# A convolution/attention trunk on one core: shorter bias rows, and LayerNorm's channel sums by pairwise additions

## What is computed

```python
# layer 0: conformer convolution module
a, b, z = split(rmsnorm(x) @ w_in)                 # 2048 channels each
u = a * sigmoid(b)
c = causal_depthwise_conv(u, conv_w, width 31) + conv_b
mu  = mean(c, over channels)
var = mean((c - mu)**2, over channels)
cn  = (c - mu) * rsqrt(var + eps) * ln_g + ln_b
x   = x + (silu(cn) * silu(z)) @ w_out
# layer 1: three attention groups (window, dilation) = (128,1), (512,4), (2048,16)
bias = rel_bias[t5_bucket(distance * dilation)]    # one value per head and distance
score = q.k * scale + bias, masked where distance < 0 or outside the window
```

## Time and profile before

| | |
|---|---|
| median of 3 runs | 1447.31 us (1447.19 to 1447.31) |
| profiled execution, own time | 1447.93 us |
| its span, first to last instruction | 1446.0 us |
| PE busy | 1427.4 us (99%) |
| DVE / ACT / POOL busy | 895.6 (62%) / 720.3 (50%) / 384.9 us (27%) |
| mean granted TensorE clock | 0.998 |
| layer 0 with its projection | about 0 to 390 us |

### The profile page before, as it was taken

The page is one execution under the profiler, slowest core; times in us unless marked ns, Lnnn a source line. Parts: engine busy times, 40 slices in busy tenths (PEclk is TensorE's granted clock), DMA queues, the critical chain, the costliest instruction groups (busy, mean ns, idle before and its releaser), DMA issues.

```text
span 1446.0 us, 23852 instructions
## 1 busy us (share of the span) xinstructions
PE 1427.4 (99%) x8915; PEld 1312.8 (91%) x8915; DVE 895.6 (62%) x1503; ACT 720.3 (50%) x1167; POOL 384.9 (27%) x169
## 2 busy tenths in 40 slices
PE   7999999999999999999999999999999999999997
PEld 6999999988889989999899998999989999899886
DVE  3899999622556566565665656656566565665633
ACT  6344444675644455444554445544455444554643
POOL 5888888798300000000000000000000000000785
PEclk9999999999999999999999999999999999999999
DMA  9676766556697666676666766667666676664652
GB/s 276 179 196 179 196 184 192 166 196 199 181 267 191 174 185 174 179 191 174 185 174 178 192 174 185 174 177 193 174 185 174 178 192 174 185 174 164 235 194 87
DMA packets 455088, 268.49 MB, mean 186 GB/s; under 512 B 4491, under 2 KB 437211, under 8 KB 454668
## 3 DMA queue, kind: packets, MB, share of 16 engines
q1 hardware_dynamic: 454572, 267.11, 65.2%
q10 hardware_dynamic: 480, 0.90, 0.2%
HBM read 263.70 MB, written 4.29 MB: 185 GB/s over the span
## 4 chain that ended last, share of the span: by engine, by line
PE 97%; ACT 1%; DVE 1%; issue 0%; ACTq 0%; DVEq 0%
PE bank L429 29%; PE bank L431 14%; PE bank L436 6%; PE bank L407 6%; PE bank L406 6%; PE bank L405 6%; PE bank L437 6%; PE bank L438 6%; PE bank L458 4%; PE bank L456 4%; PE bank L457 4%; PE bank L1463 1%; PE bank L1478 1%; PE bank L1447 1%; ACT mem_a L661 0%; PE bank L1476 0%
## 5 line engine op out<-in xcount | busy, mean ns | idle before, releaser
L370 POOL TENSOR_TENSOR w_lo<-raw,w_hi 128x1024 fp32r<-128x1024 f32 x159 | 381.5, 2409 | 1033.7 <-ACT w_hi L361 1033.3
L361 ACT ACTIVATE w_hi<-raw 128x1024 fp32r<-128x1024 f32 x382 | 399.5, 1061 | 419.7 <-PE bank L438 131.1
L370 DVE TENSOR_TENSOR w_lo<-raw,w_hi 128x1024 fp32r<-128x1024 f32 x224 | 268.4, 1222 | 187.7 <-ACT w_hi L361 185.5
L429 PE MATMUL bank<-mem_b,w_hi 128*128 128x512 f32 x1024 | 360.8, 398 | 0.0
L431 PE MATMUL bank<-mem_b,w_lo 128*128 128x256 f32 x1024 | 286.4, 280 | 0.0
L429 PE MATMUL bank<-mem_a,w_hi 128*128 128x512 f32 x768 | 270.9, 397 | 0.1
L429 PEld LDWEIGHTS bank<-mem_b,w_hi 128*128 128x128 f32 x1024 | 192.7, 188 | 45.7
L436 PE MATMUL bank<-mem_a,w_hi 128*128 128x256 f32 x768 | 216.4, 282 | 1.6 <-DVE mem_a L962 1.6
L431 PE MATMUL bank<-mem_a,w_lo 128*128 128x256 f32 x768 | 214.9, 280 | 0.0
L437 PE MATMUL bank<-mem_a,w_hi 128*128 128x256 f32 x768 | 214.8, 280 | 0.0
L438 PE MATMUL bank<-mem_a,w_lo 128*128 128x256 f32 x768 | 213.7, 278 | 0.0
(11 more groups left out here) (186 smaller groups left out, 1741.3 us busy)
## 6 DMA issues: line engine op xcount, KB each, us to landing
raw<-w_kv_dram SPq DMA_DIRECT2D x96, 1024.0 KB, 6.0
raw<-b_w_in_dram SPq DMA_DIRECT2D x64, 1024.0 KB, 7.0
raw<-a_w_in_dram SPq DMA_DIRECT2D x47, 1024.0 KB, 5.8
raw<-a_w_out_dram SPq DMA_DIRECT2D x16, 1024.0 KB, 5.0
raw<-b_w_out_dram SPq DMA_DIRECT2D x16, 1024.0 KB, 5.1
bias<-bias_dram SPq DMA_DIRECT2D x16, 384.0 KB, 6.5
x_sb<-x_dram SPq DMA_DIRECT2D x4, 512.0 KB, 5.8
resid_dram<-x_sb SPq DMA_DIRECT2D x1, 2048.0 KB, 10.0
```

Source lines behind the costliest of these rows:

```text
L361: nc.scalar.activation(w_hi[:, stream.half_slot(half), :], raw[:, slot, part:part + HALF], ACT.Copy).then_inc(hi_done, 1)
L370: eng.tensor_tensor(w_lo[:, stream.half_slot(half), :], raw[:, slot, part:part + HALF], w_hi[:, stream.half_slot(half), :].bitcast(F32), A ...
L429: nc.tensor.matmul(dst[:, :], w_hi[:, slot, k * P:(k + 1) * P], both_parts(source, kt), start=(kt == 0), stop=False)
```

## The change

The bias table has 256 columns per group, for distances 0 to 255 alone. POOL fills the whole of `bias_vec` with the mask value at its start, PE makes the rows of groups 0 and 1 in one product of 512 columns and those of group 2 in one of 256, both after slab 1, and DVE copies them between the constants in two operations, both ahead of the convolution.

The two times four reductions are replaced by eight additions of SBUF tensors each: 128x512 for the two halves of four tiles, 128x512 into the running pair of sums, and at the end 128x256. One product each remains for the mean and the variance. Each addition that needs the one before it waits for `pair_done`.

```diff
-            sp.wait_ge(vec_copied, NG)
+            sp.wait_ge(vec_copied, 2)
             sp.dma_start(bias_dram.ap(), bias_vec).then_inc(vec_stored, 16)
...
+            nc.gpsimd.memset(bias_vec, MASKED).then_inc(vec_masked, 1)
...
+            def add_channels(stat, q, tiles, done):
+                before = 7 * stat + max(0, 2 * q - 1)
+                halves = ch_sum[:, 2:4, :] if q == 0 else ch_sum[:, 0:2, :]
+                if q > 0:
+                    dve.wait_ge(pair_done, before)
+                nc.vector.tensor_tensor(halves, tiles[:, 0:2, :], tiles[:, 2:4, :], ALU.add).then_inc(pair_done, 1)
+                if q > 0:
+                    dve.wait_ge(pair_done, before + 1)
+                    nc.vector.tensor_tensor(ch_sum[:, 2:4, :], ch_sum[:, 2:4, :], ch_sum[:, 0:2, :],
+                                            ALU.add).then_inc(pair_done, 1)
+                if q == 3:
+                    dve.wait_ge(pair_done, before + 2)
+                    nc.vector.tensor_tensor(ch_sum[:, 0, :], ch_sum[:, 2, :], ch_sum[:, 3, :],
+                                            ALU.add).then_inc(done, 1)
...
-                        nc.vector.tensor_reduce(ch_sum[:, q, :], conv[:, 4 * q:4 * q + 4, :].rearrange("p k s -> p s k"),
-                                                AX.X, ALU.add).then_inc(ch_summed, 1)
+                        add_channels(0, q, conv[:, 4 * q:4 * q + 4, :], ch_summed)
...
-            def copy_vec(g):
-                dve.wait_ge(vec_made, g + 1)
-                nc.vector.tensor_copy(bias_vec[:, g * BIAS_W:(g + 1) * BIAS_W], bank[6 + g % 2][0:HEADS, :]
-                                      ).then_inc(vec_copied, 1)
+            def copy_vec(groups):
+                n = len(groups)
+                dve.wait_ge(vec_masked, 1)
+                dve.wait_ge(vec_made, groups[0] // 2 + 1)
+                by_group = bias_vec.rearrange("h (g e) -> h g e", g=NG)
+                made = bank[6 + groups[0] // 2][0:HEADS, 0:n * S].rearrange("h (g e) -> h g e", g=n)
+                nc.vector.tensor_copy(by_group[:, groups[0]:groups[0] + n, S - 1:2 * S - 1], made).then_inc(vec_copied, 1)
...
-            copy_vec(0)
-            copy_vec(1)
+            copy_vec((0, 1))
+            copy_vec((2,))
...
-                if c == 1:
-                    copy_vec(2)
...
-                nc.vector.tensor_reduce(ch_sum[:, q, :], squares[:, q, :, :].rearrange("p k s -> p s k"),
-                                        AX.X, ALU.add).then_inc(sq_summed, 1)
+                add_channels(1, q, squares[:, q, :, :], sq_summed)
...
-                for g in {1: (0, 1), 3: (2,)}.get(j, ()):
-                    if g == 2:
-                        pe.wait_ge(vec_copied, 1)
-                    nc.tensor.matmul(bank[6 + g % 2][0:HEADS, :], rel, buckets[:, g * BIAS_W:(g + 1) * BIAS_W],
-                                     start=True, stop=True).then_inc(vec_made, 1)
+                    for n, cols in enumerate((2 * S, S)):
+                        nc.tensor.matmul(bank[6 + n][0:HEADS, 0:cols], rel, buckets[:, 2 * n * S:2 * n * S + cols],
+                                         start=True, stop=True).then_inc(vec_made, 1)
...
-                    pe.wait_ge(vec_copied, NG)
-                    for q in range(4):
-                        pe.wait_ge(ch_summed, q + 1)
-                        mm = nc.tensor.matmul(bank[6][:, 0:S], mean_w[:, :], ch_sum[:, q, :], start=(q == 0), stop=(q == 3))
-                    mm.then_inc(mean_ready, 1)
+                    pe.wait_ge(vec_copied, 2)
+                    pe.wait_ge(ch_summed, 1)
+                    nc.tensor.matmul(bank[6][:, 0:S], mean_w[:, :], ch_sum[:, 0, :], start=True,
+                                     stop=True).then_inc(mean_ready, 1)
...
-                    for q in range(4):
-                        pe.wait_ge(sq_summed, q + 1)
-                        mm = nc.tensor.matmul(bank[7][:, 0:S], mean_w[:, :], ch_sum[:, q, :], start=(q == 0), stop=(q == 3))
-                    mm.then_inc(var_ready, 1)
+                    pe.wait_ge(sq_summed, 1)
+                    nc.tensor.matmul(bank[7][:, 0:S], mean_w[:, :], ch_sum[:, 0, :], start=True,
+                                     stop=True).then_inc(var_ready, 1)
```

More of the change, by code:

```diff
@@ L259, in build @@
         rel = raw[0:BUCKETS + 1, 0, NG * BIAS_W:NG * BIAS_W + HEADS]
-        buckets = raw[0:BUCKETS + 1, 0, 0:NG * BIAS_W]
+        buckets = raw[0:BUCKETS + 1, 0, 0:NG * S]
         bias_vec = gate[0:HEADS, 0:NG * BIAS_W // S, :].rearrange("p k s -> p (k s)")
@@ L281, in build @@
         rows_turned, param_ready = sem("rows_turned"), sem("param_ready")
+        vec_masked, pair_done = sem("vec_masked"), sem("pair_done")
         vec_made, vec_copied, vec_stored = sem("vec_made"), sem("vec_copied"), sem("vec_stored")
@@ L1536, in bucket_table @@
 def bucket_table():
-    table = np.zeros((BUCKETS + 1, NG, BIAS_W), np.float32)
+    table = np.zeros((BUCKETS + 1, NG, S), np.float32)
     exact = BUCKETS // 2
     for g, (window, dil) in enumerate(GROUPS):
[L1542 to L1545, removed]
+        for dist in range(S):
+            if dist % dil or dist > window:
+                table[BUCKETS, g, dist] = 1.0
                 continue
@@ L1549, in bucket_table @@
                 bucket = exact + int(math.log(dist / exact) / math.log(MAX_DISTANCE / exact) * (BUCKETS - exact))
-            table[min(bucket, BUCKETS - 1), g, e] = 1.0
-    return table.reshape(BUCKETS + 1, NG * BIAS_W)
+            table[min(bucket, BUCKETS - 1), g, dist] = 1.0
+    return table.reshape(BUCKETS + 1, NG * S)
 def kernel(**inputs):
```

## The result

| | before | after |
|---|---|---|
| median, 6 runs each on one chip | 1447.31 us (1447.07 to 1447.71) | 1453.71 us (1453.44 to 1454.01) |
| profiled execution / its span | 1447.93 / 1446.0 us | 1453.44 / 1451.6 us |
| mean granted TensorE clock | 0.998 | 0.996 |

The ratio is 1.0043, with a 95% interval of 1.0033 to 1.0053: slower by 6.4 us. The forecast was +3.8 (1451.1), its range went up to 1453.9, and the rival "POOL comes first" stood at 1453.1.

The account below looks back on a forecast made before the run. PE, busy 99% of the span, was taken as the bound. Mean +2.9 (bias advance included), clock +2.2 and variance -1.3 summed to +3.8 us, a median of 1451.1 us; range 1448.9 to 1453.9.

Parts of the forecast that it names:

- POOL comes first: Rival at the variance's fourth addition: POOL first, one more turn, PE resumes 2.9 late; +5.8 in all, 1453.1 us, chance 0.23.
- The bias rows: PE's bias products after slab 1: two in place of three, 1.59 us in place of 3.18, so -1.6 us.
- The fill, the earlier copies and the smaller load: Start of the kernel: POOL's fill, at most 2.4 us, is covered by its 11.4 us wait; copies and load cost nothing.
- The rule of turns: DVE additions with two SBUF inputs alternate with POOL operations reading SBUF: 2.8 us each where POOL waits, about 0.7 otherwise.
- The mean: Mean's three additions: sum ready at 255.60 in place of 252.71, so +2.9 us, bias advance included.
- The clock: PE's idle wait at the mean drops its clock to half about 3 us after the last product; loss 2.2 us.
- The variance: Variance's eight additions, DVE first at the fourth: PE, delayed by the clock, finds the sum ready and saves products, -1.3 us.
- Additions beside POOL: Rival: additions run beside POOL at 0.73 us each, at mean and variance; -3.7, 1443.6 us, chance 0.07.
- The clock stays up: Rival: no clock fall after the mean's wait; +2.9 + 0.6 = +3.5, 1450.8 us, chance 0.22.
- slip into POOL's pauses: Rival: some additions fall into POOL's pauses of 0.3 to 0.5 us; +1 to +2.5, about 1449.1 us, chance 0.12.
- among the taps: Additions between convolution taps meet POOL's operations; DVE ends up +0.95 against before, the last tile done at 251.60.

Follow-up runs that it names:

- experiment 1: The changed kernel with mean and variance put back to four reductions and four products each, only the shorter bias rows kept: 1445.77 us, ratio 0.9988.
- experiment 10: Shorter bias rows, channel sums kept in a PSUM bank so that additions have one input in PSUM and one in SBUF: 1443.99 us, ratio 0.9976.
- experiment 5: The changed kernel, with the variance's second addition no longer waiting for the first: 1451.91 us, ratio 1.0031.
- experiment 8: The changed kernel with unused PE products ahead of both waits, 40 at the mean and 30 at the variance: 1453.44 us, ratio 1.0042.
- experiment 9: The changed kernel without the variance's second addition's wait for the first, plus 40 unused products ahead of the mean's wait: 1451.2 us, ratio 1.0025.
- experiment 2: The changed kernel with the variance put back to four reductions and four products, additions for the mean only: 1452.5 us, ratio 1.0037.
- experiment 3: The changed kernel with the mean put back to four reductions and four products, additions for the variance only: 1450.83 us, ratio 1.0023.
- experiment 7: The changed kernel with 40 unused PE products ahead of the wait for the mean's sum: 1455.34 us, ratio 1.0056.
- experiment 6: The changed kernel with the variance's four independent additions made first, in place over the squares, then four dependent ones: 1451.45 us, ratio 1.0029.

## Why the prediction was right, and where it was off

The sign, the turns at the port and the fall of the clock were right. That the number lies inside the range is owed to the rival "POOL comes first", up to which the range had been drawn: the forecast's own sum was 2.6 us too low, and the measured 1453.71 is 0.2 below the upper end.

**The bias rows** (-1.6): 1.60 in the trace, and experiment 1 agrees. The fill, the earlier copies and the smaller load made no wait.

**The rule of turns** (2.8 us for an addition issued under POOL, 0.7 otherwise) is shown: 2.70 to 2.84 for the ones of 512 columns that POOL held up for a whole turn, and experiment 10 takes the cause away. Here the Trainium skill's page "SBUF — State Buffer", section "SBUF: two separate sides", agrees with the runs: a VectorE instruction with two SBUF inputs contends with a GpSimd operation that reads SBUF, one with at most one SBUF input does not. Beside POOL the one kind took 2.7 to 2.8 us here, the other about 0.7 (experiment 10).

**The mean** (+2.9 up to PE's release): the sum ends at 255.45, predicted 255.60, so +2.74. Each of the three additions met POOL as the prediction had it.

**The clock** (a fall some 3 us after the last product, a loss of 2.2): it fell 4.15 after, and cost 2.17 in slab products. Not counted was that the statistic's product and the entry of the next slab also run at half rate: 256.80 - 255.45 = 1.35 in place of 0.70 before, 0.65 more. That makes the +3.39, and it also delays DVE's subtraction and with it the additions of the variance.

**The variance** (-1.3) is the step that failed, in the sentence "If DVE is first, by the pattern of the earlier trace rows". I had placed the fourth addition at 260.22 and POOL at 260.23, with 0.04 us between one addition and the next. That gap was right for the third (262.84 to 262.87). The second and the fourth addition stand behind waits for `squared`, long satisfied, and for `pair_done`, and they started 0.10 and 0.11 after the end of the one before (263.56 to 263.67). The 0.12 more in all put DVE 0.11 behind POOL. The number of waits doesn't explain the longer gap: the mean's first addition stands behind two waits as well (`tap_done` and `pair_done`) and started 0.04 after its predecessor (251.52 to 251.56). What makes it stays open. POOL's own start was right: 2.20 after the first addition's, before and after. Experiment 5 took away one wait, which brought DVE forward by 0.19, turned the order round and gained 1.8 us. So the rival "POOL comes first" happened, whose sum was +2.9 + 2.9 = +5.8, the clock's loss vanishing in the wait. It did vanish, but for some 0.4 us (experiment 8).

**The sum.** In the trace 2.74 + 0.65 + 2.17 + 0.58 = +6.14 at PE, where the forecast had 3.8 and the rival 5.8; the forecast's -1.3 for the variance is 1.9 of the difference. The medians differ by 6.4, the two profiled executions by 5.5.

**The rivals.** "Additions beside POOL" is excluded by the timelines of both statistics. "The clock stays up" is excluded by the granted clock; its price with DVE first, 3.5, was 3.8 when made (experiment 9). Additions did not slip into POOL's pauses. Two among the taps read 1.92 and 1.53 in place of 2.8 because they were issued 1.0 and 1.4 us into a POOL operation, and they too end 0.55 after it; the prediction had reckoned with that (149.26 - 147.3 for the first), and the last tile was finished at 251.52 where 251.60 was predicted.

Open is why the clock fell 2.0 us after the last product once and 4.7 another time, and why it stayed low for 3.4 us in two versions (experiments 2 and 3) and 6.8 in four others (the change, experiments 5, 6 and 7). I have varied the wait, not what decides its phase, and have no theory that the runs would bear.

## What to carry to other kernels

Before a reduction is replaced by cheaper-looking additions on VectorE, look at whether both inputs lie in SBUF and whether GpSimd reads SBUF at that time; with one input in PSUM the same addition took 0.69 us in place of 2.8. Where two engines take turns, count the order at the first meeting to a tenth of a microsecond, waits included: here a shift of 0.19 us decided 1.8. And a stall of PE is to be priced with the clock that follows it, but only as far as no later wait swallows it: keeping the clock up at the mean made this kernel 1.6 us slower, since the fall then came at the variance, where it counted.

## What the runs showed of the hardware that I had not expected

- The variance's additions behind `squared` and `pair_done` start 0.10 to 0.11 us after their predecessor's end; those behind `pair_done` alone, and the mean's behind `tap_done` and `pair_done`, 0.03 to 0.04. Without the wait for the predecessor the second one starts 0.09 before its end (experiment 5).
- A POOL start 0.08 us behind DVE's left DVE first (0.69 us); one 0.11 ahead made DVE wait (2.84 us).
- A PE wait of 3.8 us was enough for the fall from 2.4 to 1.2 GHz, twice (experiments 3 and 7); waits of 1.6 us left the clock at 1.00, twice. In six versions the fall came 2.0 (experiment 7), 2.9 (6), 3.8 (3), 4.15 (the change), 4.2 (5) and 4.7 us (2) after the last product, and the half clock lasted 3.4 or 6.8 us, some of it in the wait.
